# Asking ScalarE for the table set that holds logarithm and exponential together

## The chip, the cores and the metric

One core of one Trainium2 chip runs the whole program. The metric is the device time of an execution in microseconds, the median of three runs.

## The reference, cut to what matters

Three layers act on 256 tokens of width 1024, in fp32. Layer 0 is gated linear attention (GLA), layer 1 a recurrent block (LRU); a mixture of 16 experts follows each. The third block works on 256 tokens and a context of 256 more: an mLSTM mixer, differential attention and a state-space mixer (SSD) side by side, then a convolutional feed-forward part. What the change touches:

```
rmsnorm(x, g):    x * rsqrt(mean(x*x) + eps) * g          # in every layer, per head in the mixers
modulate(h):      h * (1 + scale) + shift                 # scale, shift = silu(c) @ ada_w + ada_b
log_a  = log_sigmoid(a_lr @ w_gate_up + b_gate) / 16      # GLA gate
k_dec  = k * exp(total - cumsum(log_a));  gamma = exp(total)
g      = silu(g)                                          # GLA output gate, written with tanh
scores = sigmoid(t @ router_w)                            # router, written with tanh
a      = exp(-8 * sigmoid(.) * softplus(-lam)); mult = sqrt(-expm1(2*log_a)); gelu(gate)   # LRU
lf     = log_sigmoid(gate + bias)                         # mLSTM, with the SSD step sizes beside it
w      = exp(d_mat - m_t) * (q k^T);  h = num / max(|den|, exp(-m_t))                      # 4 heads x 2 directions
p      = softmax(q k^T * scale)                           # differential attention
```

## The kernel before, in words

Five engines have one instruction stream each, written out by hand in program order, and they meet at semaphores. The weights (390 MB) stream through a ring of SBUF slots of 1 MB; SyncE issues each load when the slot's last user has finished. Activations lie transposed, 128 rows of features by 256 tokens (512 with the context). TensorE fills PSUM banks in rotation, and each bank is read by either ScalarE (`take` in the ScalarE block, an activation from line 1377) or VectorE. TensorE waits when the bank that it wants next has not been read.

A norm in this kernel: ScalarE squares x (line 1414), TensorE sums the squares over the features with a matrix of ones (line 597), ScalarE makes the inverse norm, VectorE multiplies x by gain and inverse (line 1902), ScalarE adds the shift (line 1420), and TensorE multiplies by the next weights. `inverse` (lines 1384 to 1393) is the ScalarE part: a request for the table of Ln, a wait for the bank, the Ln from the bank into `lnt` (line 1388), and the Exp from `lnt` into `inv` (line 1392). `inverses` (lines 1395 to 1408) does several, first all the Ln (line 1401) and then all the Exp (line 1406).

ScalarE evaluates a function from the table set that is active. A load of a table set is an instruction of its own, ACT_TABLE_LOAD. There are two kinds in this program: those that the kernel asks for, `preload_act_table(ACT.Ln)` at lines 1386 and 1397, and those that the program builder puts in itself in front of an activation whose function is not in the set it takes to be active. The builder's carry the line of that activation. Copies (Identity) and Square never have a load in front.

ScalarE's order of work, with the places that matter:

- lines 1448 to 1497, start and GLA: Tanh on the condition, chunks of the modulation (`take_mod`), `inverse(D)` of the first norm at 1462, the GLA gate's softplus at 1471 and 1472, its decays by Exp at 1479 and 1480, `inverse(D)` of the context at 1490, the output gate's Tanh at 1493, and `inverses` over the four heads at 1494;
- `experts(layer)`, line 1499: `inverse(D)`, the shift, two chunks of the modulation, then the router's Tanh twice at 1505; then the experts, which use Tanh only;
- lines 1601 to 1632, LRU: `inverse(D)` at 1602, Exp at 1605, sixteen Tanh at 1614, Exp and Tanh at 1618 and 1619, Sqrt at 1623, Tanh at 1629;
- lines 1634 to 1639: the inverse of the layer stack's last norm and, right behind it, that of the third block's first norm;
- lines 1646 to 1679: gates, their softplus at 1652 and 1653, Tanh at 1671 to 1676;
- lines 1700 to 1713, the mLSTM heads: eight turns, each with an Exp floor (`m_floor`), two takes, an `inverse(SUB)` for the attention's queries and keys, four Exp of `m_exps`, and in some turns an `inverse(P)`; one more `inverse(P)` at 1713;
- lines 1716 to 1745, attention: Exp of the scores (`a_exps`), `inverse(P)` in three turns (1738) and once more at 1745, with one pair of Tanh (1744) ahead of that last one;
- lines 1746 to 1775, SSD: Tanh at 1746 and 1749, Exp at 1767 with Tanh takes between, `inverses(2, 256)` at 1775;
- lines 1777 to 1813: `inverse(D)` at 1778, then the feed-forward part with Tanh at 1809.

Of the kernel before, what the change touches and what calls it, by code (L numbers as in the profile page):

```python
# [11 lines left out]
ACT = mybir.ActivationFunctionType  # L12
# [156 lines left out]
def build(nc, A, out):  # L169
# [73 lines left out]
    SLOTS = list(plan())  # L243
    MOE_AT = [next(i for i, (what, arg) in enumerate(SLOTS) if what == "moe" and arg[0] == layer) for layer in range(2)]
    SPLIT = [g for g, (what, _) in enumerate(SLOTS) if what == "u"][:12]
    SPLIT_NTH = {g: n for n, g in enumerate(SPLIT)}
    BY_TOKEN = SPLIT[4:8]
    freed, high_used = {}, {}

    with ExitStack() as ctx:  # L250
# [5 lines left out]
        def sem(name):  # L256
            if name not in sems:
                sems[name] = ctx.enter_context(nc.semaphore(name))
            return sems[name]
# [151 lines left out]
        a_t, a_u, a_p0, a_p1, a_pt, a_o = room(TC), room(TC), room(TC), room(TC), room(2, 4, T), room(4, T)  # L411
        a_st = cond_t[:, 0:16].rearrange("p (b n) -> p b n", b=2)
        s_pad, _, s_x, s_xt = room(8, 2, 258), room(4, T), room(8, TC), room(4, 512)
        s_z = y_s
        s_zt = room(4, T)
# [68 lines left out]
        def ring_half(n, b, of=ring):  # L484

            g = SPLIT[n]
            w = of[:, g % RING, :].rearrange("p (k n) -> p k n", k=KT)
            return w[:, 4 * b:4 * b + 4, :] if g in BY_TOKEN else w[:, :, b * P:(b + 1) * P]

        def high_half(n, b):  # L490

            return (odd_high if n % 2 else even_high)[:, b].rearrange("p (k n) -> p k n",
                                                                      k=4 if SPLIT[n] in BY_TOKEN else KT)
# [870 lines left out]
        def _(act):  # L1364
# [3 lines left out]
            def a(ins, done=s["act_step"]):  # L1368

                ins.then_inc(done, 1)  # L1370
                act.wait_ge(done, c(done))

            def take(dst, src=None, func=ACT.Identity, n=T, parts=P, done=None, **kw):

                ps = tiles.read(act)
                view = ps[0:parts, 0:n] if src is None else src(ps)
                act.activation(dst, view, func, **kw).then_inc(tiles.taken, 1)  # L1377
                tiles.step()
                if done is not None:
                    act.wait_ge(tiles.taken, tiles.n)  # L1380

            inv_n = [0]

            def inverse(count, n=T, at=0):

                act.preload_act_table(ACT.Ln)
                ps = tiles.read(act)
                ins = act.activation(lnt[:, 0:n], ps[:, 0:n], ACT.Ln, bias=eps, scale=1.0 / count)  # L1388
                ins.then_inc(tiles.taken, 1)
                tiles.step()  # L1390
                act.wait_ge(tiles.taken, tiles.n)
                a(act.activation(inv[:, inv_n[0] % 4, at:at + n], lnt[:, 0:n], ACT.Exp, scale=-0.5), s["norm_inv"])
                inv_n[0] += 1

            def inverses(n, count):

                act.preload_act_table(ACT.Ln)
                first = inv_n[0]
                for i in range(n):
                    ps = tiles.read(act)  # L1400
                    act.activation(inv[:, (first + i) % 4, 0:T], ps[:, 0:T], ACT.Ln, bias=eps, scale=1.0 / count)                        .then_inc(tiles.taken, 1)
                    tiles.step()
                for i in range(n):
                    act.wait_ge(tiles.taken, tiles.n - n + 1 + i)
                    at = inv[:, (first + i) % 4, 0:T]
                    act.activation(at, at, ACT.Exp, scale=-0.5).then_inc(s["norm_inv"], 1)
                    c(s["norm_inv"])
                inv_n[0] += n
# [15 lines left out]
            def high_half_in(n, b):  # L1424

                if n >= len(SPLIT):
                    return
                g = SPLIT[n]
                if b == 0:
                    act.wait_ge(landed[g % RING], 16 * (g // RING + 1))  # L1430
                if n >= 2:
                    act.wait_ge(*high_used[n - 2, b])
                act.activation(high_half(n, b), ring_half(n, b), ACT.Identity).then_inc(sem("half_high"), 1)
# [17 lines left out]
            def take_mod():  # L1451

                n = mods_taken[0]
                mods_taken[0] += 1
                if n >= 2:
                    act.wait_ge(sem("dve_tile_ready"), marks["mod_turned", n - 2])
                take(mod_row[:, n % 2, :], n=512)

            take_mod()
            squares(lambda k: sq[:, k, 0:T], lambda k: (sem("dve_tile_taken"), marks["x_turned", k // 2]))  # L1460
            take_mod()
            inverse(D)
            take_mod()
            take_mod()
            shift_in(mods[:, 0, 0:8])
            take(g_lr[0:16, :], parts=16)
            for j in range(2):
                take(g_q[:, j, :], scale=float(P) ** -0.5)
            take_mod()
            act.wait_ge(sem("gla_neg"), 1)  # L1470
            a(act.activation(g_l, g_l, ACT.Exp))
            a(act.activation(g_l, g_l, ACT.Ln, bias=one), sem("gla_log"))
# [15 lines left out]
            for j in range(2):  # L1488
                take(g_g[:, j, :])
            inverse(D)  # L1490
            for j in range(2, 8):
                take(g_g[:, j, :], done=j == 7 or None)
            a(act.activation(sq[:, :, T:TC], g_g, ACT.Tanh, scale=0.5), sem("gla_tanh"))  # L1493
            inverses(GLA_H, GLA_DV)
            for j in range(4):
                take_mod()
            squares(lambda k: sq[:, k, 0:T], residual_in(0))

            def experts(layer):
                inverse(D)  # L1500
                shift_in(mods[:, layer, 24:32])
                take_mod()
# [145 lines left out]
            a(act.activation(decay[:, 1:2], decay[:, 0:1], ACT.Exp), sem("gate_z"))  # L1648
            for b in range(2):
                high_half_in(1, b)  # L1650
            act.wait_ge(sem("gate_neg"), 1)
            a(act.activation(z_e, z_e, ACT.Exp))
            a(act.activation(z_e, z_e, ACT.Ln, bias=one), sem("gate_log"))
# [32 lines left out]
            def m_floor(n):  # L1686

                if n >= 2:
                    act.wait_ge(sem("m_read"), n - 1)
                take(m_rc[:, 3 * (n % 2), :], func=ACT.Exp, scale=-1.0, done=True)  # L1690

            def m_exps(n):

                act.wait_ge(sem("dve_tile_taken"), marks["m_row", n])
                r = 32 * (n % 2) + n // 2
                for st in range(4):
                    e = m_e[:, n % 2, st, :]
                    act.activation(e, e, ACT.Exp, bias=col_c[:, st, r:r + 1]).then_inc(sem("m_exp"), 1)

            m_floor(0)  # L1700
            m_exps(0)
            for hd in range(M_H):
# [67 lines left out]
            for hd in range(S_H):  # L1770
                if hd + 1 < S_H:
                    s_exps(hd + 1)
                if spare:
                    spare.pop(0)()
            inverses(2, 256)

            squares(lambda k: f_sq[:, k, 0:T], residual_in(2))
# [906 lines left out]
```

## Time and profile before

| | |
|---|---|
| median of 3 runs | 1894.09 us (1893.87 to 1896.95) |
| the profiled execution, its own time | 1892.52 us |
| its span in the profile | 1890.6 us |
| granted TensorE clock over the span | 0.974 of full |
| TensorE busy / VectorE busy / ScalarE busy | 1787.2 / 1089.6 / 759.8 us |

The profile follows one execution. "Busy" is the time in which an engine had an instruction in work; the chain of waits is followed back from the last instruction, at each step to what released it. An idle time in brackets behind an instruction, as `[4.17 <-ACT inv L1392]`, is how long its engine stood still before it and what ended that.

### The profile page before, as it was taken

The page shows a single profiled execution, that of the slowest core. Times are in us where ns is not written, and L with a number is a line of the kernel's source. Part 1 is how long each engine was busy: PE and PEld are TensorE (multiplying, and loading weights), DVE is VectorE, ACT ScalarE, POOL GpSimd, SP SyncE. Part 2 cuts the span into 40 slices and gives each one's busy share as a digit, 9 for nine tenths or more (in the row PEclk, how much of TensorE's full clock was granted, in tenths as well). Part 3 has the DMA queues.
Part 4 walks back from the last instruction along what each step waited for, and adds up shares of the span by engine and source line. Part 5 has one row for each costly group of instructions (what it writes and reads, how often), then busy time and mean ns, then how long its engine had stood idle before and what let it go on. Part 6 is the DMA issues. An engine that isn't in the chain of part 4 may idle for free.

```text
span 1890.6 us, 23412 instructions
## 1 busy us (share of the span) xinstructions
PE 1787.2 (95%) x9437; PEld 1408.2 (74%) x9437; DVE 1089.6 (58%) x1593; ACT 759.8 (40%) x976; POOL 0.2 (0%) x4
## 2 busy tenths in 40 slices
PE   6999999999998989999999979999999998989998
PEld 4786777777876847777777766987645776879998
DVE  2332554447886354644468868438855563449886
ACT  3212433244664233323356665336633432034443
POOL 0000000000000000000000000000000000000000
PEclk9999899999999999999999999999989999989999
DMA  9847577668884685777778862235621322445550
GB/s 360 274 152 261 213 265 284 268 267 309 309 316 156 224 303 196 287 292 287 279 261 303 313 213 67 90 112 196 208 81 51 112 82 74 133 156 179 180 177 23
DMA packets 178596, 392.95 MB, mean 208 GB/s; under 512 B 11318, under 2 KB 102057, under 8 KB 162105
## 3 DMA queue, kind: packets, MB, share of 16 engines
q1 hardware_dynamic: 176814, 389.58, 57.8%
q10 hardware_dynamic: 1674, 1.88, 0.3%
q8 instruction: 75, 1.23, 0.3%
q14 instruction: 33, 0.26, 0.0%
HBM read 390.39 MB, written 1.05 MB: 207 GB/s over the span
## 4 chain that ended last, share of the span: by engine, by line
PE 87%; DVE 6%; ACT 4%; DMA 2%; issue 1%; SPq 0%; DVEq 0%; ACTq 0%
PE bank L849 18%; PE bank L539 12%; PE bank L877 9%; PE bank L1284 7%; PE bank L680 4%; PE bank L1086 4%; PE bank L1295 3%; PE bank L861 3%; PE bank L566 3%; PE bank L640 3%; PE bank L583 2%; DMA ring<-in_ada_w_dram 2%; PE bank L1240 2%; PE bank L892 2%; PE bank L549 1%; PE bank L597 1%
## 5 line engine op out<-in xcount | busy, mean ns | idle before, releaser
L2086 DVE TENSOR_TENSOR parts<-ring,parts 128x2048 fp32r<-128x2048 f32 x144 | 329.1, 2291 | 166.8 <-ACT parts L1527 165.7
L849 PE MATMUL bank<-parts 128*128 128x512 f32 x1536 | 369.3, 400 | 9.6 <-DVE parts L2162 4.0
L1527 ACT ACTIVATE parts<-ring 128x2048 fp32r<-128x2048 f32 x144 | 275.2, 1917 | 230.5 <-PE bank L849 164.2
L849 PEld LDWEIGHTS bank<-parts 128*128 128x128 f32 x1536 | 292.7, 193 | 79.4 <-issue 18.6
L1377 ACT ACTIVATE work<-bank 128x256 f32<-128x256 f32 (+3 forms) x223 | 97.9, 446 | 452.8 <-PE bank L539 135.8
L539 PE MATMUL bank<-hh,ring 128*128 128x256 f32 x896 | 200.7, 384 | 3.7 <-ACT hh L1420 3.7
L539 PEld LDWEIGHTS bank<-hh,ring 128*128 128x128 f32 x896 | 171.2, 192 | 32.0 <-issue 8.6
L877 PE MATMUL bank<-parts 128*128 128x512 f32 x768 | 179.4, 391 | 3.7 <-DVE parts L2111 3.7
L877 PEld LDWEIGHTS bank<-parts 128*128 128x128 f32 x768 | 143.4, 188 | 36.7 <-DVE parts L2111 4.1
L1284 PE MATMUL bank<-parts 128*128 128x256 f32 x1056 | 131.0, 286 | 7.6 <-DVE parts L2626 7.6
L1284 PEld LDWEIGHTS bank<-parts 128*128 128x128 f32 x1056 | 130.0, 196 | 8.4 <-DVE parts L2626 8.4
L1086 PE MATMUL bank<-hh,ring 128*128 128x256 f32 (+1 forms) x256 | 88.3, 498 | 2.3 <-ACT lnt L1388 1.3
L680 PE MATMUL bank<-work,ring 128*128 128x256 f32 x384 | 83.6, 380 | 2.5 <-DVE work L1831 1.4
L680 PEld LDWEIGHTS bank<-work,ring 128*128 128x128 f32 x384 | 72.7, 190 | 13.1 <-DVE work L1831 1.8
L1827 DVE TENSOR_TENSOR work<-work 128x256 f32<-128x256 f32 (+10 forms) x120 | 68.5, 571 | 19.9 <-ACT work L1619 8.3
L2626 DVE TENSOR_TENSOR parts<-ring,parts 128x2048 fp32r<-128x2048 f32 x33 | 75.5, 2291 | 7.4 <-ACT parts L1795 6.9
L1836 DVE SCALAR_TENSOR_TENSOR work<-work,cols 128x256 f32<-128x256 f32 (+1 forms) x144 | 76.2, 529 | 5.1
L1086 PEld LDWEIGHTS bank<-hh,ring 128*128 128x128 f32 x256 | 48.0, 192 | 41.6 <-issue 35.7
L1836 DVE SCALAR_TENSOR_TENSOR work<-work 128x256 f32<-128x256 f32 (+5 forms) x99 | 63.2, 638 | 27.2 <-ACT work L1493 8.7
L1414 ACT ACTIVATE work<-x 128x256 f32<-128x256 f32 x56 | 21.8, 413 | 135.6 <-DVE x L1909 126.8
L1795 ACT ACTIVATE parts<-ring 128x2048 fp32r<-128x2048 f32 x33 | 62.8, 1909 | 23.5 <-PE bank L1295 23.5
L640 PE MATMUL bank<-ring,cond 128*32 128x512 f32 x384 | 52.0, 659 | 13.9 <-DMA ring<-in_ada_w_dram 9.4
(293 smaller groups left out, 2191.4 us busy)
## 6 DMA issues: line engine op xcount, KB each, us to landing
ring<-in_moe_w_gate_dram SPq DMA_DIRECT2D x64, 1024.0 KB, 6.5
ring<-in_moe_w_up_dram SPq DMA_DIRECT2D x64, 1024.0 KB, 7.3
ring<-in_moe_w_down_dram SPq DMA_DIRECT2D x64, 1024.0 KB, 5.9
ring<-in_ada_w_dram SPq DMA_DIRECT2D x48, 1024.0 KB, 7.2
ring<-in_w_in_dram SPq DMA_DIRECT2D x32, 1024.0 KB, 5.9
ring<-in_w_mod_dram SPq DMA_DIRECT2D x24, 1024.0 KB, 7.4
ring<-in_w_up_dram SPq DMA_DIRECT2D x22, 1024.0 KB, 5.1
ring<-in_gla_w_in_dram SPq DMA_DIRECT2D x12, 1024.0 KB, 7.9
```

The lines of the kernel that those rows point to most:

```text
L539: ins = pe.matmul(ps[:, 0:n], w[:, k, m * P:(m + 1) * P], rhs(k), start=k == 0, stop=k == kt - 1)
L640: ins = pe.matmul(ps[32 * j:32 * j + 32, :], lhs, w[:, j, :], start=half == 0, stop=half == 1)
L680: ins = pe.matmul(ps[:, 0:T], w[:, k, m * P:(m + 1) * P], rhs(k), start=k == 0, stop=k == KT - 1)
L849: ins = pe.matmul(bank[:, :], xg[:, a_, k, tile * P:(tile + 1) * P], w[b_][:, j, :], start=k == 0 and n == 0, stop=k == KT - 1 and n == 2)
L877: ins = pe.matmul(y_bank(rank, b, n)[:, :], he_t[:, b, a_, q * P:(q + 1) * P], w[b_][:, j, n * 512:(n + 1) * 512], start=i == 0 and q == 0 ...
L1086: ins = pe.matmul(ps[:, 0:n], w[:, k, m * P:(m + 1) * P], rhs(k), start=k == 0, stop=k == KT - 1)
L1284: ins = pe.matmul(ps[:, 0:T], w[a_][:, k, m * P:(m + 1) * P], h_parts[:, b_, k, :], start=k == 0 and i == 0, stop=k == KT - 1 and i == 2)
L1377: act.activation(dst, view, func, **kw).then_inc(tiles.taken, 1)
L1527: act.activation(moe_w[:, n % 3, 0, :], ring[:, g % RING, :], ACT.Identity)\
L1836: v(dve.scalar_tensor_tensor(out=o, in0=i0, scalar=sc, in1=i1, op0=op0, op1=op1), done)
L2086: dve.tensor_tensor(moe_w[:, n % 3, 1, :], ring[:, (MOE_AT[layer] + AT[key]) % RING, :], moe_w[:, n % 3, 0, :].bitcast(F32), sub).then_inc ...
L2626: dve.tensor_tensor(w_parts[:, n % 3, 1, :], ring[:, (ff0 + n) % RING, :], w_parts[:, n % 3, 0, :].bitcast(F32), sub).then_inc(sem("low_re ...
```

## The change

A small helper, `log_tables`, asks for the set `natural_log_exp_and_others` by its name. It stands where `inverse` and `inverses` asked for Ln's table, and in three new places: ahead of the GLA gate's softplus, ahead of the third block's softplus, and ahead of the mLSTM heads. No activation is changed, added or moved.

```diff
+            def log_tables():
+                act.preload_act_table_set("natural_log_exp_and_others")
+
             inv_n = [0]

             def inverse(count, n=T, at=0):

-                act.preload_act_table(ACT.Ln)
+                log_tables()
                 ps = tiles.read(act)
...
             def inverses(n, count):

-                act.preload_act_table(ACT.Ln)
+                log_tables()
                 first = inv_n[0]
...
             take_mod()
+            log_tables()
             act.wait_ge(sem("gla_neg"), 1)
             a(act.activation(g_l, g_l, ACT.Exp))
             a(act.activation(g_l, g_l, ACT.Ln, bias=one), sem("gla_log"))
...
                 high_half_in(1, b)
+            log_tables()
             act.wait_ge(sem("gate_neg"), 1)
             a(act.activation(z_e, z_e, ACT.Exp))
             a(act.activation(z_e, z_e, ACT.Ln, bias=one), sem("gate_log"))
...
+            log_tables()
             m_floor(0)
             m_exps(0)
```

## Rows read from the trace of the kernel before

**Rows 1.** Page: busy us (share) x instructions, of TensorE.
```profile
PE 1787.2 (95%) x9437; PEld 1408.2 (74%) x9437; DVE 1089.6 (58%) x1593; ACT 759.8 (40%) x976; POOL 0.2 (0%) x4
```

**Rows 2.** Page: chain that ended last, share of the span by engine.
```profile
PE 87%; DVE 6%; ACT 4%; DMA 2%; issue 1%; SPq 0%; DVEq 0%; ACTq 0%
```

**Rows 3.** ScalarE's groups by line, table loads: count, busy us, mean ns, idle before.
```profile
L1386 ACT ACT_TABLE_LOAD x24 | 30.8, 1283 | 0.4
L1392 ACT ACT_TABLE_LOAD x24 | 30.8, 1283 | 0.4
...
L1406 ACT ACT_TABLE_LOAD x2 | 2.6, 1283 | 0.0
...
L1472 ACT ACT_TABLE_LOAD x1 | 1.3, 1283 | 0.0
L1479 ACT ACT_TABLE_LOAD x1 | 1.3, 1283 | 0.0
...
L1653 ACT ACT_TABLE_LOAD x1 | 1.3, 1283 | 0.0
```

**Rows 4.** Chain of waits in the last norm: start us, length us, what.
```profile
1678.17 0.47 ACT lnt L1388
...
1678.66 1.28 ACT L1392
...
1679.95 0.42 ACT inv L1392
```

**Rows 5.** Timeline, VectorE instructions that wait for an inverse norm.
```profile
596.83 2.46 DVE L1902 SCALAR_TENSOR_TENSOR hh<-x,gains,inv 128x256 f32<-128x256 f32 x6 [4.17 <-ACT inv L1392]
...
1125.86 3.25 DVE L2273 SCALAR_TENSOR_TENSOR x<-x,cols,inv 128x256 f32<-128x256 f32 x8 [1.20 <-ACT inv L1392]
...
1133.11 3.26 DVE L1902 SCALAR_TENSOR_TENSOR hh<-x,gains,inv 128x256 f32<-128x256 f32 x8 [4.00 <-ACT inv L1392]
...
1599.09 2.04 DVE L1836 SCALAR_TENSOR_TENSOR work<-work,cols,inv 128x256 f32<-128x256 f32 x4 [3.54 <-ACT inv L1406]
...
1680.47 3.25 DVE L1902 SCALAR_TENSOR_TENSOR hh<-x,gains,inv 128x256 f32<-128x256 f32 x8 [4.28 <-ACT inv L1392]
```

**Rows 6.** Timeline of the attention, TensorE behind ScalarE.
```profile
1416.35 1.96 PE L1086 MATMUL bank<-hh,ring 128*128 128x512 f32 x4 [0.64 <-ACT lnt L1388]
...
1457.28 3.78 PE L1188 MATMUL bank<-work 128*128 128x256 f32 x8 [3.96 <-ACT work L1377]
```

**Rows 7.** Stage of the heads (stretch, length, PE, PEld, DVE, ACT busy); timeline at its end.
```profile
1268.00:1362.00 94.00, 93.77 (x478) 65.79 (x479) 77.44 (x148) 60.39 (x96) 0.00 (x0) 1.00 0.51 177
...
1373.77 0.48 DVE L1836 SCALAR_TENSOR_TENSOR work<-work,cols,inv 128x256 f32<-128x256 f32 x1 [0.33 <-ACT inv L1392]
```

**Rows 8.** Timeline around the first norm.
```profile
26.27 1.92 PE L640 MATMUL bank<-ring,cond 128*32 128x512 f32 x16
...
28.61 0.60 ACT L1377 ACTIVATE work<-bank 128x512 f32<-128x512 f32 x1
...
30.30 0.13 PEld L640 LDWEIGHTS bank<-ring,cond 128*32 128x32 f32 x4 [0.30 <-DMA ring<-in_ada_w_dram]
```

**Rows 9.** Chain of waits at the end of the GLA gates.
```profile
154.07 1.92 ACT work L1493
...
157.82 1.97 PE bank L640 x16
...
160.22 7.54 DMA ring<-in_ada_w_dram
```

**Rows 10.** Timeline: router scores of layer 0, the LRU's first Tanh, the third block's gates.
```profile
205.76 3.72 PE L774 MATMUL bank<-w_router,hh 128*128 128x16 f32 x32
...
208.31 1.44 ACT L1377 ACTIVATE work<-bank 128x512 f32<-128x512 f32 x4
...
640.40 0.47 ACT L1377 ACTIVATE work<-bank,misc 128x256 f32<-128x256 f32 x1 [0.92 <-PE bank L1029]
...
1155.99 0.68 DVE L1827 TENSOR_TENSOR work<-work 128x512 f32<-128x512 f32 x1
```

## The prediction, made before the changed kernel was run

> **What bounds the kernel now.** I read the page's busy line first: TensorE is busy 95% of the span [rows 1], so what ScalarE saves can shorten the run only where TensorE stands still. Then the chain of waits by engine: ScalarE holds 4% of it [rows 2]. Third, ScalarE's groups by line, to see the table loads. There are 59: 24 at line 1386 (asked for, before the Ln), 24 at 1392 (the builder's, before the Exp), 2 and 2 for the grouped inverses, and seven single ones; four of these groups and three of the single loads stand in [rows 3], less line 1397, which is as line 1406. Each takes 1283 ns, whichever function it is for: Ln (1386, 1472, 1653) or Exp (1392, 1479). In all they are 76 us of ScalarE. Last I followed chain and timeline through every place where a load sits.
>
> A norm shows what one load costs on the chain: Ln at 1678.17 for 0.47, the load from 1678.66 for 1.28, Exp from 1679.95 [rows 4]. From the end of Ln (1678.64) to Exp is 1.31 us; the load itself starts 0.02 behind Ln, and so would Exp. So a load between them costs **1.29, say 1.3 us**.
>
> **What the change does to the loads.** Exp directly after Ln finds its function in the active set: all 24 loads at 1392 and both at 1406 go, and those at 1472, 1479 and 1653. The requests of 1386 and 1397 stay, 26 in number, and three are added. A Tanh after one of these sets must load its own again: before, it rode on Exp's set (there is no load at 1493, 1505, 1614, 1744, 1746 or 1809 before, so that set holds Tanh too). The new ones are at 1493, at 1505 in two layers, 1614, 1744, 1746 and 1809: seven. So 59 - 29 + 3 + 7 = 40 loads, 24 us less of ScalarE work. Of the 29 requests, 21 come when the set is already active (a previous inverse or softplus, no Tanh between). Nothing in the trace shows such a repeated request: it costs between 0 and 1.28 us. I take 1.28, since the call is an instruction of the kernel's own, and each of the 24 calls of `inverse` has its load in [rows 3], though none of these was a repeated one; both ends go into the cases below.
>
> The question is then what follows each of the removed loads.
>
> *Gains in full.* After the experts of layer 0, in the norm at 595 us: VectorE had been idle for 4.17 us when the inverse came. The third block's first norm at 1131: idle 4.00. Grouped inverses at 1597: 3.54. The feed-forward norm at 1679: 4.28 [rows 5]. In all four TensorE waits behind VectorE. In the attention's last `inverse(P)`, ScalarE's take behind the Exp releases TensorE, idle 3.96 us [rows 6]. The idle times exceed 1.3, so each passes on whole: 5 x 1.3 = **6.5 us**.
>
> *Gains cut off by the next wait.* The norm at 1124: VectorE was idle only 1.20 (it was busy with copies until then) [rows 5], gain 1.2. The mLSTM heads, where half of all inverses are: TensorE is busy 93.77 of 94 us [rows 7]. Eleven removed loads there are ScalarE time that TensorE never waits for, and 0.23 is all that can be won; I take 0.2. The inverse behind the heads, at 1371: VectorE idle 0.33 before it [rows 7], gain 0.3. It looks like a full site on the chain, but VectorE has its own queue to within 0.33. The first norm: ScalarE's take at 28.61 moves forward only to the end of the matmuls it reads, 26.27 + 1.92 = 28.19, and a weight slot lands by 30.30 [rows 8], so 0 to 0.4; I take 0.2, the middle, as the landing is near. Sum **1.9 us**.
>
> *No gain.* The GLA gate and its decays, the context's norm and the router norms have TensorE busy beside them; the first two `inverse(P)` of the attention release TensorE by their Ln (idle 0.64, [rows 6]), ahead of which the request still stands.
>
> *Costs.* The Tanh at 1493 is on the chain: Tanh 154.07, load and Ln of the grouped inverses, then TensorE at 157.82 for a bank, and its end frees the slot for a transfer of 7.54 us from 160.22 [rows 9]. A load before that Tanh delays all of this: **+1.3**; the removed load of 1406 comes after the Ln and gives nothing back. The router's Tanh (1505): everything on ScalarE before it is 1.3 earlier through the removed load of the same norm, and the new load uses that up: ScalarE has done its two chunks of the modulation at 209.4 (208.31 + 1.44, less two small Tanh of 0.18), when TensorE's scores (205.76 + 3.72 = 209.48) are ready [rows 10]. So 0, and up to 1.3 each if the load went behind the wait. The LRU's first Tanh at 640.40 follows 0.92 of idle time [rows 10]: 0.4 late, and taken up by the gaps between its fifteen followers. Tanh 1746 replaces the Exp load just before it: 0. Tanh 1744 and 1809, and the request before the heads, fall in idle time of ScalarE or beside a busy VectorE: 0, at most 1.3 for 1809, which has no cover that I can see whole. The request before the softplus at 1652 takes the place of the load at 1653: Ln ends as before, and VectorE takes it at 1155.99 without a pause [rows 10]: 0.
>
> **Sum.** -6.5 - 1.9 + 1.3 = **-7.1 us**. The profiled execution took 1892.52 (span 1890.6 and 1.9 around it), so it would be 1885.4; that execution was 1.6 under the median 1894.09, so the median becomes **1887.0 us**, 0.38% faster.
>
> The same page (section "What ACT_TABLE_LOAD costs") puts a switch at about 2.66 us: the load and a drain of about 1.38. The rows disagree: Exp starts 0.01 behind the load's end, and the load 0.02 behind Ln [rows 4]. By the page's figure the five full gains and the one loss would be 2.66 each, and the sum about -12.6.
>
> **Rivals.**
>
> *Repeated requests leave no load* (the builder drops them). For it: it places its own loads only where a set is missing. Against: these are the kernel's own instructions. Then 19 loads are left. Beyond the sum above, the attention's three inverses gain 0.64, 0.64 and 1.3 [rows 6], the norm at 1129 about 0.2, the others are hidden: -2.8 more, **1884.2**.
>
> *The gain is taken up behind the norms.* Weight transfers are issued when slots are free; where one lands just in time, an earlier norm only waits for it. The norms at 595 and 1679 stand ahead of stretches with dense weight traffic. With both lost, 2.6 less: **1889.6**. Against it: transfers are issued on TensorE's progress, so they move with it.
>
> *A drain with each load*, as above: five gains of 2.7, not 1.3, and so for the loss: 5.5 more, **1881.5**. Against it: [rows 4].
>
> *Tanh is in the new set.* No load at 1493: 1.3 more, **1885.7**.
>
> *Slower: Exp is not taken from the new set.* If the builder still gives each Exp its first set, every load at 1392 stays, and the three new requests come on top. Place and price: at the third block's softplus, a request and an Exp load and an Ln load follow each other where one stood, Ln ends 2.6 later, and VectorE at 1155.99, which has little to spare, starts some 2.3 late on the chain; the heads begin up to 0.4 late. It decides as soon as loads remain at 1392. +2.7: **1896.8**. Against it: an Exp after Tanh has no load of its own before, so the builder does look at the set that is active.
>
> **How the numbers follow.** Forecast 0.56, with a range of its own from 1885.5 to 1888.5 (the caps, the two cases of 0 to 1.3 and the spread of runs); repeats dropped 0.18; gain taken up 0.12; Tanh in the set 0.03; drain 0.02; Exp with its own loads 0.05; the last 0.04 for a slowdown that I don't see, such as a lower clock in a stretch. About 0.2%, 3.8 us, is what a measurement of this kernel can tell from no change. The gain taken up (4.5 us) lies near that bound, so 0.07 of it counts as faster and 0.05 as same. Faster 0.56 + 0.18 + 0.07 + 0.03 + 0.02 = 0.86; same 0.05 + 0.05 = 0.10; slower 0.04. The range from 1882.5 to 1891.0 holds the first three and the fourth.
>
> **What would show it.** Right: no loads at the lines of 1392, 1406, 1472, 1479 and 1653; 29 loads at the request itself, one for each call; loads at 1493, 1505 (at the take's line) and 1614; ScalarE busy about 735 us. From Ln to Exp 0.02 us. The stretch from the heads' start to the attention no shorter than by 0.6. The GLA part up to the output product 1.1 longer. Wrong: fewer than 35 loads (repeats dropped), any load between Ln and Exp (the slower rival), or a heads stage that gets much shorter, which would say that TensorE there did wait for ScalarE.

## The result, and the profile after

The changed kernel takes 1881.84 us, the median of 4 runs (1878.58 to 1882.56), against 1893.98 for the kernel before, 4 runs (1893.52 to 1896.95). The ratio is 0.9931, 95% interval 0.9916 to 0.9946. It is 12.1 us faster; forecast were 7.1, and the time lies 0.7 us below the range. The profiled execution took 1881.92 us, span 1880.1.

Busy line of the page of after, for [rows 1], and the chain's shares, for [rows 2]:

```profile
PE 1786.8 (95%) x9437; PEld 1409.1 (75%) x9437; DVE 1090.0 (58%) x1593; ACT 736.4 (39%) x957; POOL 0.2 (0%) x4
...
PE 87%; DVE 6%; DMA 3%; ACT 3%; issue 1%; SPq 0%; DVEq 0%; ACTq 0%
```

ScalarE is busy 736.4 us; about 735 were forecast. Its share of the chain fell from 4 to 3%. Its table loads by line, for [rows 3] (`log_tables` is line 1383, the helper of the takes 1377, the output gate's Tanh 1497):

```profile
L1383 ACT ACT_TABLE_LOAD x29 | 37.2, 1283 | 0.5
...
L1377 ACT ACT_TABLE_LOAD x4 | 5.1, 1283 | 0.1
...
L1497 ACT ACT_TABLE_LOAD x1 | 1.3, 1283 | 0.0
L1627 ACT ACT_TABLE_LOAD x1 | 1.3, 1283 | 0.0
```

29 requests, 29 loads: a request for the set that is active already costs its full 1283 ns. With the single ones (five more lines like the last two) there are 40, as forecast. Tanh does load again behind the new set. The chain in the last norm, for [rows 4]:

```profile
1669.58 0.48 ACT lnt L1391
1670.07 0.02 issue
1670.09 0.42 ACT inv L1395
```

Exp starts 0.02 us behind Ln. VectorE's waits for an inverse, for [rows 5], and TensorE's wait in the attention, for [rows 6]:

```profile
597.89 3.26 DVE L1908 SCALAR_TENSOR_TENSOR hh<-x,gains,inv 128x256 f32<-128x256 f32 x8 [2.89 <-ACT inv L1395]
...
1132.51 3.26 DVE L1908 SCALAR_TENSOR_TENSOR hh<-x,gains,inv 128x256 f32<-128x256 f32 x8 [2.72 <-ACT inv L1395]
...
1590.32 2.05 DVE L1842 SCALAR_TENSOR_TENSOR work<-work,cols,inv 128x256 f32<-128x256 f32 x4 [2.11 <-ACT inv L1409]
...
1670.61 3.26 DVE L1908 SCALAR_TENSOR_TENSOR hh<-x,gains,inv 128x256 f32<-128x256 f32 x8 [3.00 <-ACT inv L1395]
```
```profile
1452.86 2.00 PE L1188 MATMUL bank<-work 128*128 128x256 f32 x8 [2.68 <-ACT work L1377]
```

Each wait is 1.28 shorter, the grouped one 1.43. The stage of the heads, for [rows 7], is not shorter (TensorE busy in all 94 us, ScalarE 47.75 of them instead of 60.39). At the GLA gate, for [rows 9], the load stands where it was forecast, and TensorE waits 2.03 us instead of 0.75:

```profile
155.15 1.28 ACT L1497 ACT_TABLE_LOAD   x1
156.44 1.91 ACT L1497 ACTIVATE work<-work 128x2048 f32<-128x2048 f32 x1
158.38 1.28 ACT L1383 ACT_TABLE_LOAD   x1
...
160.19 5.34 PE L640 MATMUL bank<-ring,cond 128*32 128x512 f32 x32 [2.03 <-ACT inv L1404]
```

TensorE's idle time at the places of the forecast, from both traces (us):

| place | forecast | idle before | idle after |
|---|---|---|---|
| norm at 595 | -1.3 | 3.72 | 2.44 |
| norm at 1124 | -1.2 | 3.63 | 2.46 |
| norm at 1131 | -1.3 | 3.65 | 2.37 |
| heads | -0.2 | 0.23 | 0 |
| behind the heads, two waits | -0.3 | 1.32, 1.03 | 1.04, 0.73 |
| attention's last `inverse(P)` | -1.3 | 3.96 | 2.68 |
| grouped inverses, 1597 | -1.3 | 4.45 | 3.03 |
| feed-forward norm | -1.3 | 7.59 | 6.31 |
| GLA gate | +1.3 | 0.75 | 2.03 |

That is -8.5 and +1.3, -7.2 in all; without the first norm, whose 0.2 I could not read off, forecast were -6.9. So at these places the waits came out as worked out, and the time did not. Over the whole span TensorE stood still 9.3 us less, from matmul to matmul; the other 2.1 lie mainly between 680 and 750 us (-2.3), and a second trace of the changed kernel, below, does not show them. What it shows in their place stands in a column that I had not used, PEclk, the granted clock of TensorE. The windows view, 12 us around the attention's last wait, first before, then after, aligned to the take that ends the wait (stretch, length, busy us and instructions of PE, PEld, DVE, ACT, POOL, PEclk, DMA):

```profile
1452.00:1464.00 12.00, 8.04 (x26) 6.20 (x25) 5.56 (x10) 4.65 (x6) 0.00 (x0) 0.72 0.30 87
```
```profile
1447.60:1459.60 12.00, 9.32 (x41) 7.26 (x41) 5.64 (x10) 5.03 (x7) 0.00 (x0) 1.00 0.29 87
```

Before, TensorE was granted 0.72 of full: it worked part of the stretch at 1.2 instead of 2.4 GHz behind its 3.96 us of idle time. After, with 2.68 us, it had the full clock throughout. 8.04 and 9.32 are what the waits leave of 12 us; but in them 26 matmuls were done before and 41 after. Busy time does not show a slow clock, the instructions per busy us do. The reverse stands at the GLA gate: the six microseconds behind the wait have 1.00 before and 0.72 after, where the wait grew.

```profile
157.60:163.60 6.00, 5.19 (x48) 1.73 (x52) 3.51 (x7) 4.85 (x11) 0.00 (x0) 1.00 0.51 160
```
```profile
160.00:166.00 6.00, 5.80 (x36) 1.69 (x36) 4.82 (x10) 3.40 (x10) 0.00 (x0) 0.72 0.27 68
```

The start of one and the same matmul in both traces, less the idle time up to it, gives what the pace cost: -2.8 us at the attention's last wait, -1.7 behind the norm at 595, -1.7 at 1377, -0.9 in the feed-forward part; on the other side +1.7 at 35 and +1.6 at the GLA gate. Elsewhere, away from the shortened waits, it went both ways: +2.4 from 235 to 250, but -2.6 just before that, -2.9 near 475, +6.2 between 680 and 785 and -1.5 near 966. In this one pair they nearly cancel: -1.4 in all by 1880 us (clock over the span 0.974 and 0.973).

### The profile page after: what moved, and what is told of

It reads as the page before. It is cut to its first block, busy times and chain, and to the rows that moved or that the text cites. A ratio compares the mean times of both kernels' runs of the same rounds, so it can differ in the third digit from the quotient of the medians.

```text
span 1880.1 us, 23393 instructions
## 1 busy us (share of the span) xinstructions
PE 1786.8 (95%) x9437; PEld 1409.1 (75%) x9437; DVE 1090.0 (58%) x1593; ACT 736.4 (39%) x957; POOL 0.2 (0%) x4
## 4 chain that ended last, share of the span: by engine, by line
PE 87%; DVE 6%; DMA 3%; ACT 3%; issue 1%; SPq 0%; DVEq 0%; ACTq 0%
PE bank L849 18%; PE bank L539 12%; PE bank L877 9%; PE bank L1284 7%; PE bank L1086 5%; PE bank L680 4%; PE bank L1295 3%; PE bank L861 3%; PE bank L566 3%; DMA ring<-in_ada_w_dram 3%; PE bank L640 3%; PE bank L583 2%; PE bank L1240 2%; PE bank L892 2%; PE bank L549 1%; PE bank L597 1%
## 5 line engine op out<-in xcount | busy, mean ns | idle before, releaser
L680 PEld LDWEIGHTS bank<-work,ring 128*128 128x128 f32 x384 | 73.0, 191 | 12.1 <-DVE work L1837 1.8
```

The lines of the kernel that those rows point to most:

```text
L680: ins = pe.matmul(ps[:, 0:T], w[:, k, m * P:(m + 1) * P], rhs(k), start=k == 0, stop=k == KT - 1)
```

## The experiments

Two theories: W, a wait is worth its idle time; C, a wait also costs TensorE's clock behind it. All kernels were timed in five rounds, each against the kernel before on its own chip. "Pace" is, as above, how much earlier or later one and the same matmul starts, less the difference in idle time up to it.

**The changed kernel again.**

> The changed kernel once more, in five rounds. Theory W (waits): TensorE's idle time in front of the seven shortened waits is all there is; the profile pair showed 9.3 us less idle time between matmuls, so repeats lie near 9 to 10 us under the kernel before, and the spread is chance. Theory C (clock): where TensorE stood still for less time, it also ran less at the lower clock afterwards, so the ratio stays near the first one: 11 to 13 us faster, 0.9931 within 0.001, and stretches at half clock behind the attention's last inverse norm (before: 6.83 us of it, after 3.96 us of standing still) are again absent.

1882.40 us (1879.43 to 1884.41) against 1894.26; ratio 0.9932 [0.9919, 0.9944]. Every run also gives its mean granted clock. One minus this, times the span, is a rough price of the slow stretches (it counts idle time in them too): on average 53.4 us over the 22 runs of before and 47.3 over these 6. So of some 12 us about half goes with the clock, as far as this rough price tells. The trace of this run shows it. By 1880 us, against the trace of the kernel before, it has 5.1 us less idle time and 5.9 us from the pace; the first trace of the changed kernel had 9.3 and 1.4. The sum is nearly the same, 11.0 and 10.7. At the places that the change touches both traces agree (pace -1.7 at 595, -2.8 at the attention's last wait, -0.9 in the feed-forward part, +1.6 at the GLA gate). They differ mainly from 200 to 250 and from 680 to 785 us, and there the trace with more idle time has the better pace. Why the two trade there was not looked into.

**One place alone**, in the kernel before:

```diff
-            def inverse(count, n=T, at=0):
+            def inverse(count, n=T, at=0, joint=False):
...
-                act.preload_act_table(ACT.Ln)
+                if joint:
+                    log_tables()
+                else:
+                    act.preload_act_table(ACT.Ln)
...
-                        inverse(P)
+                        inverse(P, joint=hd == A_H - 1)
```

> The kernel before, with the joint set asked for in one place alone: the last inverse norm inside the attention loop. W: one load of 1.3 us goes from a wait of TensorE of 3.96 us, 1.3 us faster. C: TensorE then stands still 2.7 us and no longer falls to half clock behind it; the 24 or so matmuls at half clock gave away 2.8 us, so 4.1 us faster.

1891.02 us, ratio 0.9980 [0.9971, 0.9989]: -3.2 by the medians for a wait that is 1.28 shorter. The whole interval, -5.5 to -2.1, lies beyond W's 1.3. The wait and the window of this run's trace:

```profile
1458.31 3.56 PE L1188 MATMUL bank<-work 128*128 128x256 f32 x8 [2.68 <-ACT work L1377]
```
```profile
1453.00:1465.00 12.00, 9.32 (x34) 6.95 (x33) 5.64 (x10) 4.65 (x6) 0.00 (x0) 0.86 0.29 87
```

Here half of the slow stretch stayed (0.86, 34 matmuls): a wait of 2.68 us does not always leave the clock alone.

**All places but this one**, in the changed kernel: `inverse(P, joint=hd < A_H - 1)` and Ln's own table where `joint` is false.

> The changed kernel, with Ln's own set, as before, in that one place. W: 1.3 us slower than the changed kernel, some 10.8 faster than before. C: 4.1 us slower than the changed kernel, some 8 us faster than before, with half clock behind that norm again.

1885.04 us, ratio 0.9946 [0.9933, 0.9959]: 2.6 more than the changed kernel on the same chip. Idle time is back by 1.28 and the slow clock with it:

```profile
1453.64 3.78 PE L1188 MATMUL bank<-work 128*128 128x256 f32 x8 [3.96 <-ACT work L1377]
```
```profile
1448.40:1460.40 12.00, 8.04 (x25) 6.12 (x25) 5.59 (x10) 4.65 (x6) 0.00 (x0) 0.72 0.30 87
```

The two ratios differ by 0.0014, about the half-width of each, so that by itself the time does not part 1.3 from 4; the window does.

**A load put back between Ln and Exp**, in both helpers of the changed kernel:

```diff
                 act.wait_ge(tiles.taken, tiles.n)
+                log_tables()
                 a(act.activation(inv[:, inv_n[0] % 4, at:at + n], lnt[:, 0:n], ACT.Exp, scale=-0.5), s["norm_inv"])
```

> The changed kernel with one more request for the same set between Ln and Exp in every inverse norm and in the grouped ones: the 1.28 us is back in each, without a change of set. It tests that the whole gain is the load between Ln and Exp. If it is (W and C alike), the time is that of the kernel before plus 1.3 us for the Tanh load at the GLA output gate: about 1895. If something else in the new set gives time (its Ln, its Exp, or the rows beside them), it stays several us under 1894.

1898.43 us, ratio 1.0021 [1.0013, 1.0030]: 4.2 more than before, where 1.3 were expected. The removed loads are the source of the whole gain, since it goes when they are back. The miss, some 3 us, has two likely parts, whose sizes were not measured apart. First, what the router's Tanh cost was covered by the load that had gone from the norm ahead of it; with this one back, the new load comes behind the scores (TensorE's were ready at 209.48 in [rows 10]):

```profile
209.71 1.05 ACT L1377 ACTIVATE work<-bank 128x512 f32<-128x512 f32 x2
210.78 1.28 ACT L1377 ACT_TABLE_LOAD   x1
212.07 0.40 ACT L1377 ACTIVATE work<-bank 128x16 f32<-128x16 f32 x2
```

Second, the slow clock at the GLA gate, which this kernel shares with the changed one: its pace there is 1.6 us behind that of the kernel before.

**The wait filled too far.** TensorE gets matmuls of nothing, 128x128 into a bank that is then dropped, ahead of the attention's last wait in the kernel before:

```diff
+            def warm(to, n):
+
+                ps = to.fill(pe)
+                for _ in range(n):
+                    pe.matmul(ps[:, 0:P], ones, ident, start=True, stop=True)
...
+            warm(to_dve, 33)
             a_values(A_H - 1)
```

> The kernel before, with 33 small matmuls (128x128, written to a bank that is overwritten afterwards) put into TensorE's stream ahead of its wait behind the attention's last inverse norm, where it stood still for 3.96 us. No load, no wait and no result changes. C (clock): TensorE doesn't fall to half clock behind that wait, 2.8 us faster than before. W (waits alone): same time, 1894.3.

1896.51 against 1894.78, ratio 1.0007 [0.9996, 1.0018]: no gain. But the fillers were mis-sized. Each call took 0.228 us, together 7.53, some 3.5 more than the wait (the trace has two records for each call, 66 for 33):

```profile
1459.36 7.53 PE L593 MATMUL bank<-con 128*128 128x128 f32 x66
```
```profile
1459.00:1478.00 19.00, 19.00 (x124) 17.66 (x123) 5.64 (x10) 7.11 (x11) 0.00 (x0) 1.00 0.25 69
```

The clock stays full behind them; their excess ate what that gave. This run says nothing for W or C by its time, and was done again with fewer.

**The same with 15 fillers**, 3.4 us.

> The kernel before with 15 fillers, not 33, ahead of the attention's last wait: 33 took 7.5 us (0.228 each, not 0.11) and outlasted the wait of 3.96 by 3.5, which hid what they did to the clock. 15 take 3.4 and fit. C: no half clock behind that wait, 2.8 us faster than before. W: same as before.

1891.23 against 1893.76, ratio 0.9988 [0.9977, 0.9999]: -2.5, with every table load of the kernel before in its place and its work unchanged. This is the clock by itself. The two traces show it matmul by matmul: from 30 us to the wait this kernel runs 0.2 to 0.6 us behind the kernel before, at 1470 us it is 2.4 ahead, and from 1600 to the end 2.4 to 2.9. No other stretch moved by more than 0.6.

```profile
1453.51 3.51 PE L593 MATMUL bank<-con 128*128 128x128 f32 x30
1457.63 1.99 PE L1194 MATMUL bank<-work 128*128 128x256 f32 x8 [0.61 <-ACT work L1384]
```
```profile
1452.40:1464.40 12.00, 11.39 (x68) 10.08 (x68) 5.64 (x10) 5.04 (x7) 0.00 (x0) 1.00 0.30 87
```

68 records less 30 for the 15 fillers are 38 matmuls, about the 41 of after, and not the 26 of before.

**Tanh's load earlier**, in the changed kernel, `act.preload_act_table(ACT.Tanh)` behind the context's `inverse(D)`, where ScalarE waits for TensorE's output gate.

> The changed kernel, with Tanh's table asked for ahead of the six takes of the GLA output gate, in idle time of ScalarE, so the load leaves the chain in front of that Tanh. W: 1.3 us faster than the changed kernel. C: 2.3 us or more, since TensorE's longer wait there (2.03 against 0.75 us) was followed by half clock in both profiles of the changed kernel, and a later stretch at half clock (240 us) also grew.

1879.47, ratio 0.9920 [0.9907, 0.9933]: 15.3 less than before, against 12 for the changed kernel. On the path stand 1.3; the medians give 3, the ratios 2.1, uncertain by more than 3, so the time alone doesn't decide. The trace does: TensorE's matmuls at the gate wait 0.75 us again and have the full clock.

```profile
158.60 3.64 PE L640 MATMUL bank<-ring,cond 128*32 128x512 f32 x32 [0.75 <-ACT inv L1404]
```
```profile
158.40:164.40 6.00, 5.79 (x52) 1.77 (x52) 4.83 (x10) 3.55 (x10) 0.00 (x0) 1.00 0.52 162
```

The same 32 matmuls took 5.34 in the changed kernel. At the attention's last wait, 2.69 us here, this run's trace has 0.86, as that of the one place alone.

**No repeated requests**: `log_tables()` only where another set was active before, 8 instead of 29.

```diff
-            def inverse(count, n=T, at=0):
+            def inverse(count, n=T, at=0, ask=False):
...
-                log_tables()
+                if ask:
+                    log_tables()
```

> The changed kernel, asking for the joint set only in the 8 places where another set is active; the 21 repeated requests, 1283 ns each, are left out. W, as predicted for that case: 2.8 us faster than the changed kernel (0.64 + 0.64 + 1.3 in the attention, 0.2 at the third block's first norm). C: up to 2 us more, since the attention's last wait shrinks to 1.4 us and one low stretch in three profiles there goes too.

1877.70, ratio 0.9913 [0.9900, 0.9926], 17.1 less than before, and less than the changed kernel by 5 after the medians, by 3.4 after the ratios; W's price was 2.8.

```profile
1450.21 1.99 PE L1188 MATMUL bank<-work 128*128 128x256 f32 x8 [1.26 <-ACT work L1377]
```

The wait is 1.42 shorter than in the changed kernel, and in the attention's first two inverses the waits of 0.64 [rows 6] are gone, as the rival of the prediction had it.

**The two together.**

> The changed kernel with only the 8 needed requests and with Tanh's table asked for early at the GLA output gate. The two touch different places, so their gains add up: 4.7 (no repeats) and 2.9 (early Tanh) against the changed kernel, so 1874.5 to 1875, if the clock's share in each is bound to its place (C). By waits alone 2.8 + 1.3 = 4.1 less than 1882, so 1878.

1875.15, ratio 0.9906 [0.9889, 0.9922]: 18.6 less than before.

**Fillers in eight waits of the changed kernel**, first too many (18, 18, 18, 22, 20, 34, 24, 52), then as many as the waits hold (8, 8, 8, 10, 9, 16, 11, 25).

> The changed kernel with small matmuls, as in the first of this set, in eight of TensorE's waits: the norms at 597 and 1125 us and 1131, the one behind the heads, the attention's last, the SSD's first head, the grouped norm at 1590, the feed-forward norm. W: no change, or slower where a filler outlasts its wait. C: the stretches at half clock behind these (1133, 1369, 1499, 1591, 1676 us in the changed kernel, some 3.4 to 6.8 us each, half of it lost where TensorE works) go: 5 to 9 us faster than the changed kernel.

1891.19, ratio 0.9981 [0.9972, 0.9989]: the clock is 0.983 in the profiled run, but the fillers outlast the waits, and 9 us of the gain are lost.

> The changed kernel with fillers that fit into the eight waits (8, 8, 8, 10, 9, 16, 11 and 25 of them at 0.228 us, each set some 0.5 us shorter than its wait). C: no low stretches behind these; with the waits as they were, 5 to 8 us faster than the changed kernel. W: same as the changed kernel, 1882.

1871.71, ratio 0.9883 [0.9866, 0.9899]: 22.1 less than before, 10 less than the changed kernel, without one real instruction moved.

**The question of size, with the clock held in both kernels.** What is the change worth if TensorE does not cool down at these waits in either? The kernel before with 14, 13, 13, 10, 15, 16, 17, 31 fillers, the changed one with 8, 8, 8, 10, 9, 16, 11, 25 again:

> The kernel before with fillers in the same eight waits, each filled to some 0.5 us short of its length before (14, 13, 13, 10, 15, 16, 17, 31). With the clock held up behind these waits in both kernels, the change can only act by its waits there. If the clock made up the missing 5 us (C), this kernel is well under the kernel before (12 us or more), and the changed kernel with fillers lies only 5.5 us under it: 8.5 less idle time in eight places, some 3 more at the GLA output gate, which has no filler. If the clock had no part (W), the two differ by the full 12.

> The changed kernel with its fitted fillers once more, on the same chip as the one above, to be read as the difference of the two: C 5.5 us, W 12 us.

1880.28, ratio 0.9926 [0.9913, 0.9940], and 1872.90, ratio 0.9882 [0.9867, 0.9897]. The change is worth **7.4 us** between them by the medians, 8.3 by the ratios. W's sum of waits was 7.1; without fillers it was 12.1. One minus the clock, times the span, is now 31.2 and 32.7 us, no longer in favour of the changed kernel. The uncertainty, from both intervals, is about 4, so this agrees with the split without fixing it alone, and the 12 of W lie only just outside. The clock is held at these waits only: elsewhere it still went its own way (over the span 0.986 and 0.980 in the two profiled runs).

**All of it**: no repeated requests, Tanh early, fillers in seven waits (8, 8, 7, 10, 16, 11, 25; none at the attention's last, which is 1.26 now).

> The same with fillers in seven waits (8, 8, 7, 10, 16, 11, 25; the attention's last wait is short now). C: 5 to 7 us under the version without fillers, about 1869. W: no change from it.

1867.83 (1865.27 to 1870.27), ratio 0.9869 [0.9852, 0.9886]: 25.9 less than before, and the fastest version. From its page:

```profile
PE 1791.4 (96%) x9607; PEld 1418.0 (76%) x9607; DVE 1089.6 (58%) x1593; ACT 708.6 (38%) x936; POOL 0.2 (0%) x4
```

## Why the prediction was wrong in size

**Right:** the 40 loads and their lines, ScalarE's 735 us, 1.3 us for a load between Ln and Exp, the five full places, the caps at 1124 and in the heads, the load at the GLA gate, and the router's and the LRU's loads as hidden. The repeated request cost its 1.28. Behind the heads 0.3 was too little: two waits in a row each lost 0.3.

**The step that failed:** "The idle times exceed 1.3, so each passes on whole: 5 x 1.3 = **6.5 us**." As idle time this held (6.5 measured). As time of the kernel it lacked a term, what TensorE does behind the wait. The same step is in the costs: "A load before that Tanh delays all of this: **+1.3**"; the trace has the wait 1.28 longer and the 32 matmuls behind it 1.7 slower (5.34 against 3.64), so about 3.

Shown by experiment is the term at the attention's last wait: 15 matmuls of nothing give back 2.5 us (0.2 to 4.4) with the loads as before, and 2.8 in the pair of traces. All sixteen traces, one for each run, say how far it holds at three places (granted clock from the end of the wait for 8 us at 595 and 6 at the gate; for the attention, 12 us from 4 before it):

| place | wait, us | traces | granted clock |
|---|---|---|---|
| norm at 595 | 3.7 | 5 | 0.79 in four, 1.00 in one |
| | 2.4 | 6 | 1.00 in all |
| | 0.7 or less, with fillers | 5 | 1.00 in all |
| attention's last | 3.96 | 3 | 0.72 in all |
| | 2.7 | 4 | 1.00 in two, 0.86 in two |
| | 1.3 or less | 9 | 1.00 in all |
| GLA gate | 0.75 | 8 | 1.00 in all |
| | 2.03 | 8 | 0.72 in seven, 1.00 in one |

Two lines of the norm at 595, before and after, then the two exceptions, the one place alone at 595 and the fitted fillers at the gate:

```profile
598.10:606.10 8.00, 8.00 (x30) 6.74 (x31) 6.90 (x30) 3.20 (x9) 0.00 (x0) 0.79 0.01 2
599.10:607.10 8.00, 7.97 (x37) 7.08 (x38) 6.90 (x30) 3.66 (x10) 0.00 (x0) 1.00 0.01 2
...
600.30:608.30 8.00, 7.97 (x37) 7.06 (x38) 6.89 (x30) 3.66 (x10) 0.00 (x0) 1.00 0.01 2
...
159.00:165.00 6.00, 6.00 (x53) 1.76 (x53) 4.80 (x11) 3.33 (x9) 0.00 (x0) 1.00 0.49 147
```

So at these places a longer wait was followed by a slow stretch more often, but the length alone does not decide it. For the sum, 7.4 of the 12.1 us remain when the clock is held at the waits, so some 5 are the clock's, give or take 4; the pace of the second trace says 5.9, the runs' mean clock about 6 (53.4 against 47.3). The three places give some 2 of these net, as an average over the traces: 1.4 at 595 and 2.0 at the attention's last wait, less 1.4 at the gate. The feed-forward norm gives 0.9 in both traces of the changed kernel, but has the clock of before (0.74 and 0.75) in two of the kernels built on it. The stretch at 1377 does not go with the change: it is there again (0.77 to 0.82 in the 10 us from 1377 on) in all four kernels built on the changed one without fillers and without the load put back. Where the rest of the 5 comes from stays open.

The rows to see it in were at hand: the clock over the span was in my own table (0.974), and the windows view has it for each stretch. I had asked for some twenty of them, and 0.93 stood behind the norm at 595 and 0.89 behind that at 1131; I made nothing of these and show the view for the heads only, where the clock is 1.00 [rows 7]. The Trainium skill ("TensorE: Matmul & The Clock Gate", section "Why this matters for your kernels") warns of long idle gaps between bursts of matmuls, since the clock then falls to half; by this rule each wait near 4 us [rows 6] was to be looked at for its clock. This case's trace agrees, 0.72 behind the wait of 3.96 us; and the same 0.72 stands behind the gate's wait of 2.03 us, so here a shorter one was enough.

I had named a lower clock only as a slowdown, with 0.04. It could work in both directions, and it did: a gain at the shortened waits, a loss at the gate's longer one.

**The rivals.** The drain behind each load would have given 1881.5, next to the result, and is wrong all the same: the gaps at a load are 0.01 to 0.02 us [rows 4], and each wait shrank by 1.28, not 2.7. The nearness of a total says nothing for a mechanism. Repeated requests dropped: refuted by 29 loads, and worth 3 to 5 us where it is done by hand. Gain taken up: the norms at 595 and 1679 kept theirs. Tanh in the set: refuted by line 1497. Exp with its own loads: none at 1395.

## What to carry to other kernels

Price a wait of TensorE twice: its idle time, and the granted clock in the few microseconds behind it (instructions per busy us tell, busy time does not). Here a wait of 4 us that became 2.7 returned more than it was shortened by, and one that grew from 0.75 to 2 cost more. One trace of each kernel was not enough to see its size, since slow stretches come and go between executions of one kernel. Where a wait can't be removed, a few matmuls of nothing that end before it does bring most of this back, and if they outlast it, they cost more than they bring. Ask for a table set by name where Ln and Exp alternate, and only where another set was active.

## What the hardware did that was not expected

A request for the set already active costs 1283 ns, as any load (29 of 29). A 128x128 fp32 matmul with its weight load took 0.228 us as a filler (7.53 us for 33). Some 22 us of fillers (95 by 0.228) in idle time of the changed kernel gave back 10 us; and the clock around equal waits of 2.68 us was 1.00 in two kernels' traces and 0.86 in two others'.
